# Layer 1's conditioning product in blocks of 512 columns instead of 256, on VectorE

## The reference

```python
mods = jnp.split(jax.nn.silu(cvec) @ lp['w_ada'] + lp['b_ada'], 6, axis=-1)   # w_ada: 2048 x 12288
sh1, sc1, g1, sh2, sc2, g2 = [m[:, None, :] for m in mods]
h = rms_norm(x, lp['g_pre1']) * (1.0 + sc1) + sh1
...                                        # attention, pooling and convolution heads, merged by w_out
x = x + g1 * rms_norm(mix, lp['g_post1'])
h = rms_norm(x, lp['g_pre2']) * (1.0 + sc2) + sh2
f = jnp.square(jax.nn.relu(h @ lp['w_mlp1'])) @ lp['w_mlp2']
x = x + g2 * rms_norm(f, lp['g_post2'])
```

## Time and profile before

| | us |
|---|---|
| median of three runs | 3561.15 (3559.43 to 3568.66) |
| the profiled execution's own time | 3564.84 |
| its span, first to last instruction | 3562.8 |
| PE busy | 3271.1 (92%) |
| DVE busy | 2207.7 (62%) |
| ACT busy | 1202.7 (34%) |
| POOL busy | 664.7 (19%) |

### The profile page before, as it was taken

One profiled execution on the slowest core, in us unless ns is written; L12 is line 12 of the kernel. 1 busy time (PEld: TensorE's weight loads), 2 busy tenths in 40 slices (PEclk: granted clock), 3 DMA queues, 4 the chain that ended last, 5 costly groups with the idle time before them and its releaser, 6 DMA issues.

```text
span 3562.8 us, 51188 instructions
## 1 busy us (share of the span) xinstructions
PE 3271.1 (92%) x17787; PEld 2856.7 (80%) x17787; DVE 2207.7 (62%) x3500; ACT 1202.7 (34%) x1751; POOL 664.7 (19%) x385
## 2 busy tenths in 40 slices
PE   5899978979999999999996997787999999999998
PEld 2587755768989889889885996566998998998997
DVE  1367644389899889998888496546334344334334
ACT  2122333243333333333334323444333333333332
POOL 0047000022121221121211192002111111111110
PEclk7799999989999999999998998998999999999999
DMA  8855455636666667665662332122444444344342
GB/s 289 290 189 180 155 195 183 213 124 200 197 217 212 195 195 225 199 206 188 219 197 93 127 107 80 48 70 67 130 124 130 127 125 130 124 130 128 122 133 95
DMA packets 479418, 566.33 MB, mean 159 GB/s; under 512 B 17688, under 2 KB 395152, under 8 KB 478896
## 3 DMA queue, kind: packets, MB, share of 16 engines
q1 hardware_dynamic: 476992, 560.02, 49.2%
q0 software_dynamic: 1344, 4.33, 0.4%
q10 hardware_dynamic: 944, 0.32, 0.0%
HBM read 560.93 MB, written 3.67 MB: 158 GB/s over the span
## 4 chain that ended last, share of the span: by engine, by line
PE 65%; DVE 15%; issue 9%; ACT 5%; DMA 4%; SPq 0%; DVEq 0%; ACTq 0%; POOL 0%; POOLq 0%
PE ps L1331 33%; PE ps L1339 26%; DVE ada_sums L1258 6%; DMA ada_raw<-in_w_ada_dram 4%; DVE w_lo L816 2%; PE ps L1412 2%; ACT w_hi L541 1%; DVE conv L1027 1%; DVE h_lo L907 1%; ACT prob L713 1%; PE ps L1442 1%; ACT facc L582 1%; PE ps L1563 1%; PE ps L1360 1%; PE ps L1537 1%
## 5 line engine op out<-in xcount | busy, mean ns | idle before, releaser
L816 DVE TENSOR_TENSOR w_lo<-raw,w_hi 128x1024 fp32r<-128x1024 f32 x660 | 916.2, 1392 | 884.4 <-ACT w_hi L541 871.7
L541 ACT ACTIVATE w_hi<-raw 128x1024 fp32r<-128x1024 f32 x672 | 710.3, 1057 | 1420.5 <-PE ps L1331 703.7
L1331 PE MATMUL ps<-h_hi,w_hi 128*128 128x384 f32 x2816 | 956.6, 340 | 28.4 <-DVE h_lo L907 24.5
L1331 PE MATMUL ps<-h_lo,w_hi 128*128 128x384 f32 x2816 | 947.6, 336 | 0.0
L1331 PE MATMUL ps<-h_hi,w_lo 128*128 128x384 f32 x2816 | 947.4, 336 | 0.0
L1258 DVE SCALAR_TENSOR_TENSOR ada_sums<-ada_raw,cond,ada_sums 128x256 f32<-128x256 f32 x1440 | 649.4, 519 | 0.0
L1339 PE MATMUL ps<-w_hi,hid_hi 128*128 128x512 f32 x1536 | 606.4, 395 | 9.7 <-DVE hid_lo L1241 7.7
L1339 PE MATMUL ps<-w_hi,hid_lo 128*128 128x512 f32 x1536 | 603.5, 393 | 0.0
L1339 PE MATMUL ps<-w_lo,hid_hi 128*128 128x512 f32 x1536 | 602.7, 392 | 0.0
L1331 PEld LDWEIGHTS ps<-h_hi,w_hi 128*128 128x128 f32 x2816 | 533.8, 190 | 46.6 <-issue 40.2
L1331 PEld LDWEIGHTS ps<-h_lo,w_hi 128*128 128x128 f32 x2816 | 533.6, 189 | 0.9
(11 more groups left out here) (192 smaller groups left out, 2321.5 us busy)
## 6 DMA issues: line engine op xcount, KB each, us to landing
raw<-in_w_mlp_dram SPq DMA_DIRECT2D x512, 512.0 KB, 3.9
ada_raw<-in_w_ada_dram SPq DMA_DIRECT2D x384, 512.0 KB, 4.8
raw<-in_w_in_dram SPq DMA_DIRECT2D x96, 512.0 KB, 4.4
raw<-in_w_out_dram SPq DMA_DIRECT2D x64, 512.0 KB, 4.1
out_dram<-x SPq DMA_DIRECT2D x6, 512.0 KB, 2.7
x<-in_x_sample_dram SPq DMA_DIRECT2D x1, 2048.0 KB, 9.8
pw_w<-in_w_conv_pw_dram POOLq DMA_DIRECT2D x2, 1024.0 KB, 5.9
x<-in_x_prompt_dram SPq DMA_DIRECT2D x1, 1024.0 KB, 4.9
```

The costliest lines, as they stand in the source:

```text
L541: nc.scalar.activation(w_hi[:, j % 4, :, :], raw[:, j % 4, :, :], ACT.Copy).then_inc(hi_ready, 1)
L816: nc.vector.tensor_tensor(w_lo[:, j % 4, :, :], raw[:, j % 4, :, :], w_hi[:, j % 4, :, :].bitcast(F32), ALU.subtract).then_inc(lo_ready, 1)
L1331: last = nc.tensor.matmul(ps[:, 2 * pair + t, 0:TOK], w[:, j % 4, k, P * t:P * t + P], v[:, kt + k, :], start=begin and k == 0 and i == 0, ...
```

## The change

Layer 1's conditioning is cut into 24 blocks of 512 columns, three in each chunk. A block takes two of the old places: its upper 1024 rows are the products of an even b, its lower 1024 those of the next odd b. A piece j is now two tiles of 128 rows by 512 columns, still 512 KB, read in rows of 2 KB instead of 1 KB. DVE issues four instructions of 512 columns for each piece. ada_sums has one buffer, of the same size in all; the first product of a block waits until PE has turned the block before. The turns are three in a chunk, in quads 2, 5 and 7 (WIDE_TURN), of eight matmuls (16 passes) each, after the second unit of the quad instead of the third; in the last chunk quad 7's stands where it did. wide_mods adds the bias to four columns of mods at a time. Waits on mods_ready elsewhere count to the new number (MODS_END). Layer 0's conditioning is untouched.

```diff
+ADA_WIDE = 6 * D // NC
+MODS_END = (ADA_BLOCKS, ADA_BLOCKS + ADA_WIDE)
+WIDE_TURN = {2: 0, 5: 1, 7: 2}
...
-        ada_sums = new("ada_sums", [2, 2, UC])
+        ada_sums = new("ada_sums", [2, NC])
...
+            def load_ada_wide(ch, b, j):
+                sp.wait_ge(ada_used, ch * 24 + (4 * (ADA_BLOCKS + b) + j - 3))
+                src = w_ada[1, 1024 * (b % 2) + 2 * P * j:1024 * (b % 2) + 2 * P * j + 2 * P, bass.ds(ch * (3 * NC) + b // 2 * NC, NC)]
+                sp.dma_start(wide(ada_raw, j), src.rearrange("(k p) n -> p k n", p=P)).then_inc(ada_landed[j], 16)
...
                             if first and k % 4:
-                                load_ada(1, ch * 6 + ADA_OF_QUAD[k], j)
+                                load_ada_wide(ch, ADA_OF_QUAD[k], j)
...
+            def wide_mods(block):
+                dve.wait_ge(ada_turned, block + (ADA_BLOCKS + 1))
+                nc.vector.tensor_tensor(mods[:, 1, bass.ds(block * 4, 4), :],
+                                        ps[:, BANK_ADA, MOD:MOD + 8].rearrange("p (t g) -> p t g", g=2),
+                                        pb[:, 1, bass.ds(block * 4, 4)].unsqueeze(2).to_broadcast([P, 4, 2]),
+                                        ALU.add).then_inc(mods_ready, 1)
...
-                def ada_products(ch, block, j, mark0):
-                    n, k0 = ch * 6 + (ADA_BLOCKS + block), mark0 + 28 * block + 7 * j
+                def ada_products(ch, b, j, mark0):
+                    n, k0 = ch * 6 + (ADA_BLOCKS + b), mark0 + 3 * (4 * b + j)
+                    begin = b % 2 == 0 and j == 0
                     dve.wait_ge(ada_landed[j], 16 * (n + 1))
-                    if j == 0:
-                        dve.wait_ge(ada_turned, n - 1)
-                    for o in range(8):
+                    if begin:
+                        dve.wait_ge(ada_turned, ch * 3 + (ADA_BLOCKS + b // 2))
+                    for o in range(4):
                         k, g = divmod(o, 2)
-                        out = ada_sums[:, block % 2, g, :]
-                        if o == 1 and j:
-                            dve.wait_ge(ada_used, 4 * n + j)
-                        elif o > 1 or j:
-                            dve.wait_ge(dve_chain, k0 + (o - 1 if o > 1 else 0))
-                        if j or k:
-                            op = nc.vector.scalar_tensor_tensor(out=out, in0=ada_raw[:, j, k, :], scalar=cond[:, 4 * j + k, g:g + 1],
-                                                                in1=out, op0=ALU.mult, op1=ALU.add)
+                        out, src, by = ada_sums[:, g, :], wide(ada_raw, j)[:, k, :], cond[:, 8 * (b % 2) + 2 * j + k, g:g + 1]
+                        if o >= 2:
+                            dve.wait_ge(dve_chain, k0 + (o - 1))
+                        elif not begin:
+                            dve.wait_ge(*((ada_used, 4 * n + j) if o else (dve_chain, k0)))
+                        if begin and k == 0:
+                            op = nc.vector.tensor_scalar(out, src, by, None, ALU.mult)
                         else:
-                            op = nc.vector.tensor_scalar(out, ada_raw[:, j, k, :], cond[:, 4 * j + k, g:g + 1], None, ALU.mult)
-                        op.then_inc(ada_used if o == 7 else dve_chain, 1)
+                            op = nc.vector.scalar_tensor_tensor(out=out, in0=src, scalar=by, in1=out, op0=ALU.mult, op1=ALU.add)
+                        op.then_inc(ada_used if o == 3 else dve_chain, 1)
...
-                        if first and k in ADA_OF_QUAD and j == 3:
-                            m = ch * 6 + ADA_OF_QUAD[k]
-                            ada_mods(1, m, m + ADA_BLOCKS)
+                        if first and k in WIDE_TURN and j == 3:
+                            wide_mods(ch * 3 + WIDE_TURN[k])
...
-            def turn_sums(n, buffer):
-                pe.wait_ge(ada_used, 4 * n + 4)
-                pe.wait_ge(mods_ready, n)
-                for t in range(2):
+            def turn_sums(block):
+                pe.wait_ge(ada_used, block * 8 + (4 * ADA_BLOCKS + 8))
+                pe.wait_ge(mods_ready, block + ADA_BLOCKS)
+                for t in range(4):
...
-                        if first and k and j == 2:
-                            turn_sums(ch * 6 + (ADA_OF_QUAD[k] + ADA_BLOCKS), ADA_OF_QUAD[k] % 2)
+                        if first and k in WIDE_TURN and j == 1:
+                            turn_sums(ch * 3 + WIDE_TURN[k])
...
                 def last_beside(n, j):
-                    if first and n and (j == 2 or n == 3):
-                        k = 4 + n
-                        turn_sums(ch * 6 + (ADA_OF_QUAD[k] + ADA_BLOCKS), ADA_OF_QUAD[k] % 2)
+                    if first and 4 + n in WIDE_TURN and (j == 1 or n == 3):
+                        turn_sums(ch * 3 + WIDE_TURN[4 + n])
```

More of the change, by code:

```diff
@@ L458, in _ @@
                 nc.gpsimd.memset(glu[:, :, C_HALF + CONV_OUT:CONV_PAD], 0.0).then_inc(pads_ready, 1)
-                pool.wait_ge(mods_ready, ADA_CU if layer == 0 else 2 * ADA_BLOCKS)
+                pool.wait_ge(mods_ready, ADA_CU if layer == 0 else MODS_END[1])
                 chain.link(nc.gpsimd.memset(masks[:, :, :], 0.0))
@@ L1001, in _ @@
                 first = layer == 0
-                n_mods = ADA_BLOCKS * layer
                 with dve.Fori(0, 2) as i:
@@ L1202, in first_half @@
                     return facc[:, place(n), t, :] if n < 2 else mix_t[:, n - 2, t, :]
-                dve.wait_ge(mods_ready, n_mods + (ADA_OUT - 4 if first else ADA_BLOCKS))
+                dve.wait_ge(mods_ready, ADA_OUT - 4 if first else MODS_END[1])
                 gate_coef(1, layer, G1, G_POST1)
@@ L1284, in _ @@
                     for k in range(Q_CHUNK):
-                        mlp_quad(i, k, i * 168 + n0)
+                        mlp_quad(i, k, i * 72 + n0)
                 if not last_layer:
-                    dve.wait_ge(mods_ready, ADA_BLOCKS + 2 * DT)
+                    dve.wait_ge(mods_ready, ADA_BLOCKS + 2 * DT * P // NC)
                     scale_coef(0, layer + 1, SC1, G_PRE1)
-                n1 = n0 + ch * 168 if first else chain.n
+                n1 = n0 + ch * 72 if first else chain.n
                 def other_chunks(n, t):
@@ L1305, in _ @@
                 if first:
-                    chain.n = n0 + CHUNKS * 168
+                    chain.n = n0 + CHUNKS * 72
                 def last_mods():
-                    n = CHUNKS * 6 - 1
-                    ada_mods(1, n, n + ADA_BLOCKS)
+                    wide_mods(ADA_WIDE - 1)
                 if not last_layer:
@@ L1434, in ada_beside @@
                     ada_turn(m + 1)
-            def turn_sums(n, buffer):
-                pe.wait_ge(ada_used, 4 * n + 4)
-                pe.wait_ge(mods_ready, n)
-                for t in range(2):
+            def turn_sums(block):
+                pe.wait_ge(ada_used, block * 8 + (4 * ADA_BLOCKS + 8))
+                pe.wait_ge(mods_ready, block + ADA_BLOCKS)
+                for t in range(4):
                     for g in range(2):
-                        last = nc.tensor.matmul(ps[:, BANK_ADA, MOD + 2 * t + g:MOD + 2 * t + g + 1], ada_sums[:, buffer, g, P * t:P * t + P],
+                        last = nc.tensor.matmul(ps[:, BANK_ADA, MOD + 2 * t + g:MOD + 2 * t + g + 1], ada_sums[:, g, P * t:P * t + P],
                                                 ones[:, 0:1], start=True, stop=True)
@@ L1527, in _ @@
                 pe.wait_ge(rope_landed, 48 * (layer + 1))
-                pe.wait_ge(mods_ready, ADA_MIX if first else DEPTH * ADA_BLOCKS)
+                pe.wait_ge(mods_ready, ADA_MIX if first else MODS_END[1])
                 for i in range(2):
@@ L1657, in _ @@
                                      lambda t: pe.wait_ge(acc_copied, ch * 12 + (84 * layer + 3 * n + t + 1)), acc_done)
-                            if first and n and j == 2:
-                                turn_sums(ch * 6 + (ADA_OF_QUAD[k] + ADA_BLOCKS), ADA_OF_QUAD[k] % 2)
+                            if first and k in WIDE_TURN and j == 1:
+                                turn_sums(ch * 3 + WIDE_TURN[k])
                 ch, r = CHUNKS - 1, 2 * layer + 1
```

## The result

The changed kernel takes 3570.88 us (median of 10 runs, 3566.96 to 3577.46); the kernel before takes 3563.09 us beside it (10 runs). The ratio is 1.0021, with a 95% interval of 1.0012 to 1.0029: slower by about 7.5 us, inside the 0.3% that I had called "same". The profiled execution took 3568.39 us, its span 3566.6 us. The forecast was 3562 us.

What follows compares the result with a forecast made beforehand. TensorE's matmuls were taken to bound each chunk, with 9 to 14 us of turns, waits and half clock winnable. Seven chunks +2.5 us and the last -2 gave 3565.3 profiled, 3562 us timed, range 3543 to 3576.

Steps and rivals of the forecast that it cites:

- rival A: The forecast itself: quad 7's wait stays and the clock falls nearly each time; 3562 us, range 3553 to 3572, chance 0.45.
- Part 1: DVE's conditioning products: four wide for eight narrow, 3.79 us a unit instead of 4.30, about 11.5 us a chunk saved.
- Part 2: PE's turns, merged and one unit earlier: near 5.5 us a chunk still; stalls 0.2 us at quad 2, 0.1 at quad 5.
- Part 3: Single buffer, quad 5's turn to quad 7's: DVE 35.5 us against PE 32.7, so PE waits 2.9 us at quad 7.
- quiet chunk: A looped chunk of layer 0's MLP without a fall of the clock: forecast 141.1 us, as today.
- Part 4: TensorE's clock halves after quad 7's wait in all seven chunks, 2.6 us each; the 1.4 us of the 145.7 us chunks go.
- rival C: Quads 2 and 5 stall 1 us or more, each stall also bringing half clock: 3575 to 3590 us, chance 0.15.
- late start of 2.77 us: DVE's delay on "issue" starting the 145.7 us chunks, costing PE 1.4 us more waiting; forecast no longer to reach PE.
- Part 6: Last chunk: 1 us less waiting at its last turn and 1 us less at DVE's adds, 2 us, bounds 0 and 4.
- The sum: First seven chunks of layer 0's MLP 1007.5 us against 1005.0, +2.5; last chunk -2; timed forecast 3562 us.
- Rival B: Clock falls in none to three chunks, by longer turns or chunks in step with the clock's granting: 3544 to 3552, chance 0.27.

Runs made afterwards that it cites:

- experiment 2: Changed kernel with all three turns of a looped chunk after the third unit (last chunk's quad 5 too), buffer single: 3561.71 us, ratio 0.9994.
- experiment 3: Changed kernel with turns reading x instead of the sums, so DVE need not wait for the buffer: 3557.74 us, ratio 0.9991.
- experiment 4: Changed kernel with POOL's add of the down quads cut to one column of each 512: 3528.68 us, ratio 0.9901 to the kernel before.
- experiment 8: Changed kernel with half a turn, four matmuls (eight passes) instead of eight: 3528.73 us, ratio 0.9899 to the kernel before.
- experiment 1: Changed kernel with only quad 7's turn one unit later in the looped chunks: 3529.38 us, ratio 0.9911 to the kernel before.
- experiment 5: Changed kernel with looped turns late, quads 2 and 5 after the third unit, quad 7 after the fourth: 3520.35 us, ratio 0.9876.
- experiment 7: Kernel before (narrow products, two buffers) with every turn after the second unit instead of the third: 3623.18 us, ratio 1.0162.
- experiment 9: Kernel before (narrow products, two buffers) with the turns of quads 3 and 7 after the fourth unit: 3526.09 us, ratio 0.9891.
- experiment 6: Kernel before with only quad 7's turn after the fourth unit instead of the third in looped chunks: 3537.37 us, ratio 0.9922.

## Why the prediction was right, and where it was off

The time came 9 us above the forecast, within the range and within rival A's own (to 3572), near its upper end. The account, by its steps:

Part 1 held: 3.79 us a unit, 0.80 for the two beginning products (1288.22 to 1289.02), DVE down by 110 us or 13.8 a chunk, where I had 11.5.

Part 2: 1.84 us a turn, as said (1.94 where it began 0.13 us behind DVE's last product). Quad 2's stall was 0.16 us in each looped chunk (forecast 0.2), quad 5's none that the trace lists (0.1).

Part 3 held in its figures. DVE from turn to turn 35.3 us (35.5), its wait 0.97 (1), PE's wait 2.74 to 2.76 in six chunks and 2.14 in one (2.9). Experiments 2, 3 and 4 showed the three parts of it: the race, the buffer, POOL. With the adds short, the wait was gone, 2.8 us a chunk. The Trainium skill, "SBUF — State Buffer", section "Who interferes with whom", says that a VectorE instruction with two inputs in SBUF contends with a GpSimd instruction that reads SBUF, and calls this an exclusive lock. The runs agree: wide products were held for 3.25 us an add (5.98 less 2.73), as narrow ones were (6.50 less 3.25). The quiet chunk took 984.9 / 7 = 140.7 us where I had 141.1; the 0.4 us are the stalls, (6 x 2.75 + 2.14) / 7 + 0.16 = 2.8 us and not 3.2.

Part 4 is the step that was mis-sized, in what the clock costs: "a fall in each of seven chunks, 2.6 us each", 18.2 us. The number of falls at quad 7 was right, but six of them were 6.8 us long, so 3.2 each (22.1 in all); and the turns of quads 2 and 5 brought three more, 5.1 together. 27.2 instead of 18.2 us. The last is half of rival C, at a price I had tied to the wrong condition: I wanted a stall of 1 us before a fall there, and 0.16 us or less was enough. What part 4 let go did go: three chunks before had a wait of 1.32 us at quad 3, and none has one after. The reason was another: part 4 counted on DVE's spare time to hide the late start of 2.77 us, and no wait of DVE on "issue" is left in the seven chunks (10.0 us in four before). No run shows why. All waits of PE at turns together fell from 25.9 to 19.7 us, 6.2 of the 6.7 us that the rest of the seven chunks gained.

Part 6: -4.3 us for -2, just outside its bounds of 0 and 4. The last turn waits 0.73 us instead of 2.33, and the matmuls after DVE's adds 0.53 instead of 1.27 and 0.68: 3.0 us less. Another 1.7 us are a fall of the clock behind the last turn, from 1908.0 to 1911.4, which did not come after the change; part 6 had no term for it. DVE waited 2.1 us at the longest for quad 5's turn (2.5).

The sum: +2.5 became +9.6, by 9.0 of falls, 0.9 of the slow start and -2.8 of the quiet chunks. The last chunk gave 2.3 us more than said, so the stage took 5.2 us more where 0.5 was forecast. The profiled executions are 3.55 us apart for another reason: the stage began 5.2 us earlier after the change (756.09 instead of 761.31) and ended at 1923.15 in both, and what follows, with nothing changed in it, took 3.8 us longer. Its start lay between 750.65 and 762.11 in the other profiles, with nothing changed ahead of it. That the time came within the range therefore owes something to terms that cancel: the clock cost 9 us more than said, and the quiet chunks and the last one 5 us less.

Rival B, fewer falls, did not come: there were ten instead of four. It also spoke of falls coming in step with something else, and no run tested that. What decides whether a wait of 2.8 us before eight passes brings a fall stays open: it did in four chunks of seven before, and in seven of seven in experiment 8.

Where did 110 us of VectorE go? Into nothing. DVE was never the bound of a chunk; it was late above all at one place, 2.8 us, because of where the turn stood, and the change moved that turn earlier by about what it made DVE faster. It also tied DVE to quad 5's turn by the single buffer. Either of the two is enough to keep most of the wait: with the old place and the single buffer (experiment 2) 2.14 us were left, with the early place and no wait for the buffer (experiment 3) 2.14 us too. Both taken back at once, with wide products, was not run. Moving the turns of the kernel before, two conditions in two lines, gives 38 us; the change with late turns gives 43.

## What to carry to other kernels

When an engine waits once in each round for another that is faster on average, ask first where the consumer stands in the program's order: a unit of delay costs nothing if nobody needs the result, and here it was worth 38 us where halving the instructions was worth some 5 us more, perhaps less. A single buffer ties both engines to one event and makes the stretch between two hand-overs a race; sum both sides from that event, holds by a third engine included. Price a stall before a row of small matmuls with the clock it brings down: here 2.8 us of waiting cost 6 us.

## What was unexpected of the hardware

- A fall of the granted clock lasted 3.4 or 6.8 us, nothing else, in the seven chunks of the seven kernels that I read in windows of 1 us (before, after, experiments 1, 2, 5, 7, 8), but for the start of the stage; it cost half of that, 1.7 or 3.4 us.
- Behind a wait of 0.16 us, 16 one-column matmuls (1.94 us) were followed by the half clock in six chunks of seven in experiment 1 and two of seven in the changed kernel. The same matmuls without a wait (1.84 us) were followed by none in 21 turns of experiment 5. Eight of them (1.02 us) behind a wait of 0.27 us brought none in experiment 9.
- VectorE's delay on "issue" at the start of a chunk was up to 2.8 us in four chunks of the kernel before and 4.9 to 6.0 us in six chunks of experiments 6 and 9, but there was none in experiment 7, which is narrow too. Of the wide kernels only the one with half a turn had it, 1.0 to 1.2 us in four chunks. Its cause is not shown.
- In VectorE's products twice the columns cost 1.7 times: 0.66 us from start to start for 512, 0.396 for 256. The two tensor_scalar of a block went from 0.26 to 0.40 us each.
